# Routing one-hots of two expert layers: who makes the rows, ScalarE and VectorE or GpSimd and VectorE

## The reference, cut to what matters

```python
def chunk_fn(xc):                      # 256 tokens, 8 heads, 16 picks per head
    ...
    i1 = jnp.take_along_axis(si[:, :, 0], ci // PEER_TOPK, axis=-1)
    i2 = jnp.take_along_axis(si[:, :, 1], ci % PEER_TOPK, axis=-1)
    eidx = i1 * PEER_NKEYS + i2        # one of 128 x 128 experts
    w = jax.nn.softmax(cv, axis=-1)
    u = u_tab[eidx]
    a = jax.nn.gelu(jnp.einsum('td,thkd->thk', xc, u, preferred_element_type=f32)) * w
    return jnp.einsum('thk,thkd->td', a.astype(v_tab.dtype), v_tab[eidx])
```

## Time and profile before

| | before |
|---|---|
| median of 3 runs | 3178.33 us (3175.43 to 3185.26) |
| profiled execution, its own time | 3174.83 us |
| its span | 3173.2 us |
| busy: TensorE matmul / VectorE / ScalarE / GpSimd | 2938.2 / 2081.0 / 1487.8 / 60.5 us |
| mean granted TensorE clock | 0.967 of full speed |

### The profile page before, as it was taken

The page is one execution under the profiler, slowest core; times in us unless marked ns, Lnnn a source line. Parts: engine busy times, 40 slices in busy tenths (PEclk is TensorE's granted clock), DMA queues, the critical chain, the costliest instruction groups (busy, mean ns, idle before and its releaser), DMA issues.

```text
span 3173.2 us, 54128 instructions
## 1 busy us (share of the span) xinstructions
PE 2938.2 (93%) x18026; PEld 2613.6 (82%) x18026; DVE 2081.0 (66%) x3950; ACT 1487.8 (47%) x2826; POOL 60.5 (2%) x118
## 2 busy tenths in 40 slices
PE   5898999989999789999999999898799999999998
PEld 4688878778879579999998888785599998988886
DVE  3324895348965657887986666524368888966665
ACT  0103554234543244446985555304234449955554
POOL 0000110001100000000000000000000000000000
PEclk9899999999999889999999999988899999999999
DMA  5135984449955145554336555541155553356663
GB/s 163 61 106 163 295 338 131 133 117 342 382 166 172 47 120 173 184 180 159 105 106 195 194 193 192 129 133 27 31 177 184 181 181 101 106 172 192 193 194 114
DMA packets 312348, 518.24 MB, mean 163 GB/s; under 512 B 36673, under 2 KB 213185, under 8 KB 311618
## 3 DMA queue, kind: packets, MB, share of 16 engines
q1 hardware_dynamic: 295842, 456.78, 45.5%
q0 software_dynamic: 16416, 60.30, 5.2%
HBM read 515.97 MB, written 1.05 MB: 163 GB/s over the span
## 4 chain that ended last, share of the span: by engine, by line
PE 82%; ACT 7%; DVE 5%; issue 3%; DMA 2%; ACTq 1%; SPq 0%; DVEq 0%
PE ps L879 30%; PE ps L807 10%; PE ps L808 10%; PE ps L811 10%; PE ps L741 3%; PE ps L782 3%; PE ps L856 2%; DMA tile_ring<-mlp_w_in 2%; ACT spread L1685 1%; PE ps L752 1%; ACT spread L1691 1%; PE ps L765 1%; ACT hot_pair L1685 1%; PE ps L1289 1%; PE ps L1211 1%
## 5 line engine op out<-in xcount | busy, mean ns | idle before, releaser
L807 PE MATMUL ps<-x_high,w_high 128*128 128x256 f32 x3200 | 798.3, 287 | 44.5 <-ACT w_high L1494 25.8
L808 PE MATMUL ps<-x_low,w_high 128*128 128x256 f32 x3200 | 789.9, 284 | 0.0
L807 PEld LDWEIGHTS ps<-x_high,w_high 128*128 128x128 f32 x3200 | 617.4, 193 | 49.9 <-ACT w_high L1494 28.0
L1836 DVE TENSOR_TENSOR w_low<-tile_ring,w_high 128x512 fp32r<-128x512 f32 x688 | 470.3, 691 | 270.9 <-ACT w_high L1534 179.3
L808 PEld LDWEIGHTS ps<-x_low,w_high 128*128 128x128 f32 x3200 | 618.2, 193 | 0.1
L811 PE MATMUL ps<-x_high,w_low 128*128 128x256 f32 x3200 | 450.0, 283 | 0.0
L879 PE MATMUL ps<-w_high,x_high 128*128 128x512 f32 x1376 | 425.7, 391 | 20.1 <-DVE x_low L1831 20.1
L879 PE MATMUL ps<-w_high,x_low 128*128 128x512 f32 x1376 | 425.3, 390 | 0.0
L879 PE MATMUL ps<-w_low,x_high 128*128 128x512 f32 x1376 | 424.8, 390 | 0.0
L1665 ACT ACTIVATE w_high<-tile_ring 128x1024 fp32r<-128x1024 f32 x256 | 269.7, 1054 | 314.7 <-PE ps L811 314.2
L811 PEld LDWEIGHTS ps<-x_high,w_low 128*128 128x128 f32 x3200 | 414.1, 193 | 0.0
(11 more groups left out here) (325 smaller groups left out, 3219.3 us busy)
## 6 DMA issues: line engine op xcount, KB each, us to landing
tile_ring<-peer_u SPq DMA_DIRECT2D x256, 512.0 KB, 3.2
tile_ring<-peer_v SPq DMA_DIRECT2D x256, 512.0 KB, 4.2
arena<-mod_w POOLq DMA_DIRECT2D x112, 512.0 KB, 5.6
tile_ring<-mlp_w_in SPq DMA_DIRECT2D x64, 512.0 KB, 5.5
tile_ring<-mlp_w_out SPq DMA_DIRECT2D x64, 512.0 KB, 5.5
tile_ring<-ret_w_in SPq DMA_DIRECT2D x48, 512.0 KB, 3.9
tile_ring<-peer_w_q SPq DMA_DIRECT2D x32, 512.0 KB, 4.1
tile_ring<-sb_w_qkv SPq DMA_DIRECT2D x24, 512.0 KB, 3.8
```

The lines of the kernel that those rows point to most:

```text
L807: nc.tensor.matmul(dst, cols, x_high[:, c, :], start=c == 0, stop=False)
L808: nc.tensor.matmul(dst, cols, x_low[:, c, :], start=False, stop=False)
L1836: return V.tensor_tensor(w_low[:, k % 2, cols], tile_ring[:, k, cols], w_high[:, k % 2, cols].bitcast(F32), ALU.subtract)
```

## The change

`minus` and its two instructions in each layer go away. ScalarE makes no rows: `rows_of` on ScalarE, its semaphores and its waits go, and its 8 iterations are one loop again. VectorE makes one row of every lot (before: one of an even lot, two of an odd lot) and the columns. GpSimd makes the rows 1, 2 and 3 of every lot with the instruction that VectorE has at L2445. Its program is written out without a loop, 64 lots in each layer; it waits for `slots` once in each layer, and from lot 2 on for TensorE to have finished the lot two before. TensorE waits for `pool_row_hot` where it waited for `act_row_hot`.

```diff
-ACT_ROWS = (3, 2)
+POOL_ROWS = 3
...
-        minus = spread[:, 0:2 * T].rearrange("p (k t) -> p k t", t=T)
...
             pool.dma_start(ret_const, I["ret_const"]).then_inc(ret_loaded, 16)
+            for l in range(2):
+                u0 = UNITS[f"weigh{l}"]
+                pool.wait_ge(unit_taken, u0)
+                for g in range(T // HOT):
+                    if g >= 2:
+                        pool.wait_ge(unit_done, u0 + g - 1)
+                    for k in range(HOT - POOL_ROWS, HOT):
+                        t = HOT * g + k
+                        ins = nc.gpsimd.tensor_scalar(hot_row[g % 2][:, k, :], iota, slots[:, 0, t:t + 1], slots[:, 2, t:t + 1],
+                                                      ALU.is_equal, ALU.mult)
+                    ins.then_inc(pool_row_hot, 1)
...
-                    pe.wait_ge(act_row_hot, j * (2 * RING) + (l * T // HOT + g + 1))
+                    pe.wait_ge(pool_row_hot, j * (2 * RING) + (l * T // HOT + g + 1))
...
-                def rows_of(j, g):
-
-                    own = range(HOT - ACT_ROWS[g % 2], HOT)
-                    for k in own:
-                        ins = A(hot_row[g % 2][:, k, :], iota, ACT.Abs,
-                                bias=minus[:, 0, bass.ds(j * (2 * HOT * RING) + (HOT * g + k), 1)])
-                    ins.then_inc(row_diff, 1)
-                    act.wait_ge(row_diff, j * (2 * RING) + (l * T // HOT + g + 1))
-                    for k in own:
-                        tok_k = bass.ds(j * (2 * HOT * RING) + (HOT * g + k), 1)
-                        ins = A(hot_row[g % 2][:, k, :], hot_row[g % 2][:, k, :], ACT.Relu, bias=slots[:, 2, tok_k],
-                                scale=minus[:, 1, tok_k])
-                    ins.then_inc(act_row_hot, 1)
-
-                def weigh_tiles(j, ahead=True):
+                def weigh_tiles(j):
                     for k in range(RING):
                         high(WEIGH_FROM + k + 2, j)
                         gelu_apart(WEIGH_FROM + k, j)
-                        for b in range(2):
-                            if k + 1 < RING or ahead:
-                                act.wait_ge(unit_done, j * (2 * RING) + (u0 + 2 * k + b + 1))
-                                rows_of(j, 2 * k + b + 2)
...
-                act.wait_ge(unit_taken, u0)
-                rows_of(0, 0)
-                rows_of(0, 1)
-                n_it = T // (2 * HOT * RING)
-                with act.Fori(0, n_it - 1) as j:
+                with act.Fori(0, T // (2 * HOT * RING)) as j:
                     weigh_tiles(j)
-                weigh_tiles(n_it - 1, ahead=False)
...
                 def lift_slots(i, u):
                     z = bank(u)[:, 0:3 * P].rearrange("p (k t) -> p k t", t=P)
-                    V.tensor_scalar(minus[:, :, i * P:(i + 1) * P], z[:, 0:3:2, :], -1.0, None, ALU.mult).then_inc(dve_step, 1)
-                    settle()
                     return V.tensor_copy(slots[:, :, i * P:(i + 1) * P], z)
...
-                    for k in range(HOT - ACT_ROWS[g % 2]):
+                    for k in range(HOT - POOL_ROWS):
                         ins = V.tensor_scalar(hot_row[g % 2][:, k, :], iota, slots[:, 0, bass.ds(t + k, 1)],
                                               slots[:, 2, bass.ds(t + k, 1)], ALU.is_equal, ALU.mult)
                     ins.then_inc(row_hot, 1)
```

More of the change, by code:

```diff
@@ L391, in build @@
         row_hot = sem("row_hot")
-        row_diff = sem("row_diff")
-        act_row_hot = sem("act_row_hot")
+        pool_row_hot = sem("pool_row_hot")
         out_ready = sem("out_ready")
```

## The result

The changed kernel takes 3288.51 us in the median of 4 runs (3285.92 to 3292.62), the kernel before beside it 3177.31 us: a ratio of 1.0346, with a 95% interval of 1.0325 to 1.0367. It is slower, by 111 us where the prediction said 42, and the time lies inside the range that it gave (3155 to 3330) though far from its middle. Of each kernel one execution was profiled: 3174.83 us before, 3285.92 us after.

What follows compares the result with a forecast made beforehand. It took ScalarE's late rows to bound the weigh stage by a small margin, TensorE and VectorE close behind. Loop steps +38.6, last iterations +5.6, start -2.6: +41.6 us on 3174.8, or 3220 us median, range 3155 to 3330.

Steps and rivals of the forecast that it cites:

- The price of a GpSimd row: Weigh stage, six rows a step: 0.44 us each taken, with 0.26 and 0.78 as ends; no row showed it.
- Who pays for the exclusion: Weigh stage: GpSimd rows and VectorE's two-SBUF-input instructions exclude each other, adding 0.72 us per lot to VectorE's step.
- My formula: Weigh step: the larger of 4.91 and 4.41 + 6r - 1.20 us, for a GpSimd row of r us.
- Both start waits: Start of the weigh stage: TensorE's 0.96 and 0.34 us waits for ScalarE go, 2.6 us gained in all.
- removing `minus`: VectorE at the start of the stage: nothing gained, or 1.8 us if its cover were gone.
- The step of the kernel before: Weigh loop before the change: 19 steps in 97.95 us, so 5.16 us a step.
- The signs named for being right: Weigh stage: no TensorE wait for ScalarE, VectorE's columns, row, merge and low longer or farther apart, steps 5.6 to 6.1 us.
- The first rival: Every weigh step: GpSimd is hidden and TensorE sets the pace, -16.6 us, 3162 us median; chance 0.36.
- The second, slow GpSimd: Every weigh step: rows above 0.82 us make TensorE wait; at 0.88, +6 us, or +205 with exclusion; chance 0.14.
- The floor of 4.91 us: TensorE's weigh step without waits, read from the iteration after the loop; gain at most 0.25 us a step, 14.0 us.
- the limit of a hidden row: Weigh stage: GpSimd by itself fits up to 4.91 / 6 = 0.82 us a row within TensorE's step.

Runs made afterwards that it cites:

- e1: The changed kernel, with VectorE reading iota for its columns and its row from a copy in PSUM: 3222.6 us, ratio 1.014.
- e2: As e1, and VectorE's merge and low in the weigh loop work on 8 columns only, leaving out work: 3165.15 us, ratio 0.995.
- e7: As e2, but VectorE's low in the loop is replaced by a full-width copy with one SBUF input: 3182.7 us in one execution.
- e5: The changed kernel with two rows of a lot on GpSimd and two on VectorE: 3166.95 us, ratio 0.9944.
- e4: The kernel before, with each lot's rows split as VectorE one, GpSimd one, ScalarE two: 3152.73 us, ratio 0.9906.
- e8: The changed kernel with 4 unused constant products added on TensorE between the lots of each loop step: 3277.1 us, ratio 1.0304.
- e6: The changed kernel with 8 unused constant products added on TensorE between the lots of each loop step: 3258.9 us, ratio 1.0249.

## Why the prediction was wrong

The direction and the place were right, and so was the premise that a GpSimd row and a VectorE instruction with two SBUF inputs get in each other's way. Two steps failed. They pull in opposite directions, and it is luck that the time still lies in the range.

*The price of a GpSimd row failed.* I took 0.44 us with 0.26 and 0.78 as ends; it is 0.78 to 0.79, the upper end itself. The reasoning "one pass over 128 elements there as on VectorE" is what was wrong: each of the two parts, 0.36 us fixed and 0.43 us by column, is more than the 0.34 us that VectorE takes for the whole instruction. The Trainium skill, GPSIMD Engine Reference, section Engine selection, says one-input work runs at roughly line rate; the 0.43 us by column here, for two operations, is four times the 0.11 that I estimated from it, and the measurement decides.

*Who pays for the exclusion failed.* The prediction put the hold-ups on VectorE's step, "4.41 + 2 x 0.72 = 5.85 us". VectorE pays about 0.1 us a step, over its columns, row, merge and low: in the changed kernel the columns of the odd lots have a shortest, median and longest duration of 680, 683 and 823 ns.

```profile
L2427 DVE TENSOR_TENSOR hot_pair<-keep,spare x64: 680/683/823, 1484.9 to 2886.6; 128x512 f32<-128x512 f32 x64
```

GpSimd pays. The right sum is made on its side: 6 x 0.78 = 4.68, about 1.9 of hold-ups and 0.36 of waits for TensorE give 6.94 us, against 6.97 and 6.86 in the two layers. My formula with the right price gives 7.89 us and +168; with my wrong price 5.85 and +42. The first error made the forecast too small, the second made it too large. With the right payer and 0.44 us a row, the sum is an estimated 2.64 + 1.9 = 4.5 us, under TensorE's pace, and the change would have been a gain; no run has such a row. On the Trainium skill, SBUF — State Buffer, section Who interferes with whom: e1, e2 and e7 agree on which VectorE instructions conflict, two SBUF inputs and also a one-input copy. It also has the one that comes second wait until the first has finished. For GpSimd the trace nearly agrees: 1.10 us lost beside one low, and about the rest of the VectorE instruction wherever a row starts inside one. For VectorE it does not: columns that start inside a row are at most 0.14 us longer, and the copy of e7 0.18.

*Point by point.* Both start waits went: the first lots ran at 1487.30 and 1488.19 with none. ScalarE fell to 22.60 x 6.97 / 120 = 1.31 us a step, inside "1 to 1.5". What removing `minus` did can't be read: the first lot starts anywhere from 1485.71 (e1) to 1491.38 (e5) in the runs without it. The step of the kernel before was read a little short: from even lot to even lot 19 steps take 98.37 us, 5.18 each and not 5.16. The signs named for being right were half seen: TensorE waits for GpSimd, but the columns, the row and low are no longer than before, and the step is outside 5.6 to 6.1 us. The first rival, GpSimd hidden, needed no exclusion and less than 0.82 us a row; e2 comes close to that case, at 3165 us against its 3162. The second, slow GpSimd, was half true. The floor of 4.91 us was too high by 0.26, and with e4's 4.65 us the limit of a hidden row is 4.65 / 6 = 0.775 us, so a row of 0.78 is just past it, as the short waits in e2 show. The clock was not in the sum; it fell to 0.86, and the runs with it back at 1.00 are 11 us (e8) and 30 us (e6) below, with 20 us of GpSimd's waits gone in both.

## What to carry to other kernels

Before work is moved to GpSimd beside a busy VectorE, count on its side: the price alone times the number, plus what VectorE's instructions with two SBUF inputs hold it up, for each row about what is left of such an instruction when the row starts; VectorE itself need not slow down to make the move a loss. A split is worth trying at several sizes: three rows of four cost 3.5%, two gained 0.6% with ScalarE free, and one, with two on ScalarE, gained 0.9%. Where one engine must share, one operand read from PSUM instead (e1) took back 66 of the 111 us, part of it by the clock.

## What was not expected of the hardware

Adding 1.8 us of useless products to each step of TensorE made the kernel 30 us faster: 20 us of GpSimd's waits for TensorE went, with the granted clock at 1.00 instead of 0.86, and 6 us of hold-ups, since GpSimd then met VectorE at slightly better times. The clock fell where TensorE had waited 2.5 us in every second step, and stayed at 1.00 in e8, where it waited 1.5 us and 0.3 us in turn. The hold-up is one-sided: a GpSimd row that starts inside a VectorE instruction with two SBUF inputs takes longer by about the rest of it, while a VectorE instruction that starts inside a row is hardly longer. And a step with no wait listed for the matmuls can still hold a gap: the step of 4.91 us is 0.26 us longer than one of e4, and only the weight loads print a part of it.
